# Latent attention: the values take the probabilities' low part last, two weight splits stand behind the heads, and the output projection begins within the last head

## The reference, cut to what matters

```python
def mla_attention(hn, w_dq, q_norm_g, w_uq, w_o, k_nope, k_rope, v, cos, sin):
    ...
        sc = (jnp.einsum('bqhd,bkhd->bhqk', qn, k_nope, preferred_element_type=jnp.float32)
              + jnp.einsum('bqhr,bkr->bhqk', qr, k_rope, preferred_element_type=jnp.float32)) * scale
        q_chunk = (start + jnp.arange(Q_BLOCK)) // CHUNK
        mask = key_chunk[None, :] <= q_chunk[:, None]
        sc = jnp.where(mask[None, None], sc, -jnp.inf)
        p = jax.nn.softmax(sc, axis=-1).astype(v.dtype)
        return jnp.einsum('bhqk,bkhd->bqhd', p, v)
    ...
    return o @ w_o
```

## Time and profile before

| | |
|---|---|
| median of 3 timed runs | 1744.71 us (1744.37 to 1747.96) |
| profiled execution, whole time | 1743.44 us |
| its span on the core | 1741.5 us |
| mean granted clock of TensorE | 0.997 |
| TensorE busy | 1711.8 us, 98% of the span |
| VectorE busy | 942.6 us, 54% |
| ScalarE busy | 608.1 us, 35% |

### The profile page before, as it was taken

The page is one execution under the profiler, slowest core; times in us unless marked ns, Lnnn a source line. Parts: engine busy times, 40 slices in busy tenths (PEclk is TensorE's granted clock), DMA queues, the critical chain, the costliest instruction groups (busy, mean ns, idle before and its releaser), DMA issues.

```text
span 1741.5 us, 21892 instructions
## 1 busy us (share of the span) xinstructions
PE 1711.8 (98%) x8088; PEld 1367.2 (79%) x8088; DVE 942.6 (54%) x1264; ACT 608.1 (35%) x894; POOL 185.2 (11%) x158
## 2 busy tenths in 40 slices
PE   9989999999999999999999999999999999999998
PEld 7768888888888866477888888888777788888886
DVE  5675546652665389857532343365873754234432
ACT  4553434431444232254321222243453432122221
POOL 0210211100111101110200011100000021001111
PEclk9999999999999999999999999999999999999999
DMA  6111223332223245311332323212211233322221
GB/s 231 62 53 56 85 82 97 96 121 88 93 87 107 84 136 158 100 63 59 121 97 97 93 92 97 94 60 86 72 37 34 74 109 98 97 86 96 97 83 48
DMA packets 48883, 157.84 MB, mean 91 GB/s; under 512 B 7088, under 2 KB 7728, under 8 KB 48816
## 3 DMA queue, kind: packets, MB, share of 16 engines
q1 hardware_dynamic: 48288, 155.45, 27.8%
q10 hardware_dynamic: 528, 1.46, 0.3%
HBM read 146.14 MB, written 2.10 MB: 85 GB/s over the span
## 4 chain that ended last, share of the span: by engine, by line
PE 90%; DVE 5%; ACT 2%; issue 1%; SPq 1%; DMA 0%; POOL 0%; DVEq 0%; ACTq 0%; POOLq 0%
PE bank L1133 26%; PE bank L1134 26%; PE bank L1135 26%; PE bank L1284 1%; PE bank L1669 1%; PE bank L1290 1%; PE bank L1285 1%; DVE cv L2281 1%; PE bank L1223 1%; DVE w_lo L1910 1%; SPq L484 1%; DVE swa_p L2013 1%; PE bank L1177 1%; PE bank L1839 1%; ACT w_hi L676 0%
## 5 line engine op out<-in xcount | busy, mean ns | idle before, releaser
L1910 DVE TENSOR_TENSOR w_lo<-w_raw,w_hi 128x1024 fp32r<-128x1024 f32 x269 | 347.3, 1292 | 313.0 <-ACT w_hi L676 190.1
L1133 PE MATMUL bank<-a_hi,w_hi 128*128 128x512 f32 x1156 | 460.6, 398 | 0.1
L1134 PE MATMUL bank<-a_lo,w_hi 128*128 128x512 f32 x1156 | 456.5, 395 | 0.0
L1135 PE MATMUL bank<-a_hi,w_lo 128*128 128x512 f32 x1156 | 454.3, 393 | 0.0
L1134 PE MATMUL bank<-g_lo,w_hi 128*128 128x512 f32 x688 | 272.0, 395 | 0.0
L1133 PE MATMUL bank<-g_hi,w_hi 128*128 128x512 f32 x688 | 270.8, 394 | 0.0
L1135 PE MATMUL bank<-g_hi,w_lo 128*128 128x512 f32 x688 | 269.0, 391 | 0.0
L1133 PEld LDWEIGHTS bank<-a_hi,w_hi 128*128 128x128 f32 x1156 | 218.1, 189 | 55.9 <-issue 6.0
L1135 PEld LDWEIGHTS bank<-a_hi,w_lo 128*128 128x128 f32 x1156 | 218.1, 189 | 48.5
L1134 PEld LDWEIGHTS bank<-a_lo,w_hi 128*128 128x128 f32 x1156 | 218.5, 189 | 46.4 <-issue 1.0
L676 ACT ACTIVATE w_hi<-w_raw 128x1024 fp32r<-128x1024 f32 x153 | 159.8, 1050 | 163.8 <-PE bank L1135 150.7
(11 more groups left out here) (290 smaller groups left out, 1807.6 us busy)
## 6 DMA issues: line engine op xcount, KB each, us to landing
w_raw<-in_stream SPq DMA_DIRECT2D x269, 512.0 KB, 3.5
shifted<-u_pad SPq DMA_DIRECT2D x120, 66.0 KB, 2.0
h<-in_xT SPq DMA_DIRECT2D x8, 256.0 KB, 5.5
out<-h SPq DMA_DIRECT2D x8, 256.0 KB, 2.1
cst_b<-in_consts SPq DMA_DIRECT2D x1, 896.0 KB, 9.7
cst_b<-in_consts ACTq DMA_DIRECT2D x1, 896.0 KB, 6.3
shifted<-u_pad ACTq DMA_DIRECT2D x8, 66.0 KB, 2.4
tap_cols<-in_vectors SPq DMA_DIRECT2D x16, 29.2 KB, 1.8
```

Source lines behind the costliest of these rows:

```text
L1133: pe.matmul(out, w0, x0, start=start, stop=False, skip_group_check=loose)
L1134: pe.matmul(out, w0, x1, start=False, stop=False, skip_group_check=loose)
L1135: return pe.matmul(out, w1, x0, start=False, stop=stop, skip_group_check=loose)
L1910: dve.tensor_tensor(w_lo[slot][:, :], w_raw[slot][:, :], f(w_hi[slot][:, :]), ALU.subtract)\
```

## The change

Three things are done. In `mla_values` the matmuls that read only `pt_hi` come first and wait for ScalarE's `pt_hi` parts (`mla_ea`); the four that read `pt_lo` come last and wait for VectorE's (`mla_ev`). The splits of the "wo" units 2 and 3 leave heads 1 and 2 and stand behind head 7. And tile 0 of the output projection is begun within head 7: slices 0 to 3 ahead of the transposes, slices 4 to 6 between these and the values; behind the values come slices 0 to 6 of tile 1, slice 7 of tile 0 and slice 7 of tile 1, then tiles 2 to 7 one after another.

```diff
@@ ScalarE
-                if i in (1, 2):
-                    w_hi_of(UNIT0["wo"] + i + 1, (UNIT0["wo"] + i + 1) % RING)
...
-            after("wo", "post1", 1, 1)
+            w_hi_of(UNIT0["wo"] + 2, (UNIT0["wo"] + 2) % RING)
+            after("wo", "post1", 1)
@@ TensorE
             def mla_values(i):
                 pe.wait_ge(x_ready, SPLIT0["mla"] + i)
+                w = slice(i * P, (i + 1) * P)
+                for kt in (0, 1, 3, 2):
+
+                    pe.wait_ge(mla_ea, 3 * i + mla_cols[kt][0] - 4)
+                    c = mla_cols[kt][2]
+                    pe.matmul(bank[4][:, kt * P:], T(v_hi, kt, MLA_H * V_DIM)[:, w], pt_hi[:, c:c + SEQ - kt * P],
+                              start=(kt == 0), stop=False, skip_group_check=True)
+                    pe.matmul(bank[4][:, kt * P:], v_lo(kt)[:, w], pt_hi[:, c:c + SEQ - kt * P],
+                              start=False, stop=False, skip_group_check=True)
                 for kt in (0, 1, 3, 2):
 
                     pe.wait_ge(mla_ev, 3 * i + mla_cols[kt][0] - 4)
                     c = mla_cols[kt][2]
-                    w = slice(i * P, (i + 1) * P)
-                    last = three(bank[4][:, kt * P:], T(v_hi, kt, MLA_H * V_DIM)[:, w], v_lo(kt)[:, w],
-                                 pt_hi[:, c:c + SEQ - kt * P], pt_lo[:, c:c + SEQ - kt * P], kt == 0, kt == 2, True)
+                    last = pe.matmul(bank[4][:, kt * P:], T(v_hi, kt, MLA_H * V_DIM)[:, w],
+                                     pt_lo[:, c:c + SEQ - kt * P], start=False, stop=(kt == 2), skip_group_check=True)
                 last.then_inc(mla_pv, 1)
+
+            def wo_part(j, k0, k1):
+
+                n = UNIT0["wo"] + j
+                if k0 == 0:
+                    unit_ready(n)
+                    pe.wait_ge(mla_exp, NB * (MLA_H - 1) + j + 1)
+                for k in range(k0, k1):
+                    k_ready("mla", k)
+                    last = three(bank[j][:, :], T(w_hi[n % RING], k, P), T(w_lo[n % RING], k, P),
+                                 T(mo_hi, k), T(mo_lo, k), k == 0, k == KD - 1)
+                if k1 == KD:
+                    last.then_inc(unit_used, 1)
...
+                else:
+                    wo_part(0, 0, 4)
                 mla_transpose(i)
                 if i + 1 < MLA_H:
                     mla_scores(i + 1, 3)
+                else:
+                    wo_part(0, 4, KD - 1)
                 mla_values(i)
-            tiles("wo", 8, mo_hi, mo_lo, "mla")
+            wo_part(1, 0, KD - 1)
+            wo_part(0, KD - 1, KD)
+            wo_part(1, KD - 1, KD)
+            for j in range(2, KD):
+                n = UNIT0["wo"] + j
+                unit_ready(n)
+                if j < 4:
+                    pe.wait_ge(mla_exp, NB * (MLA_H - 1) + j + 1)
+                else:
+                    bank_free("wo", j)
+                tile_of_eight(n, n % RING, bank[j % 4][:, :], mo_hi, mo_lo)
@@ VectorE
-                if i in (1, 2):
-                    lo_ahead(UNIT0["uv"] + i)
                 x_lo(SPLIT0["mla"] + i, mo_lo, mo_hi, i, bank[4][:, :])
+            lo_ahead(UNIT0["wo"] - 1)
             for k in range(KD):
                 n = UNIT0["wo"] + k
-                if k:
-                    lo_ahead(n)
+                lo_ahead(n)
                 unit_done(n)
```

## The result

The changed kernel takes 1728.69 us (median of 4 runs, 1727.27 to 1730.44); the kernel before took 1744.54 us (median of 4, 1742.32 to 1747.96). The ratio is 0.9908, 95% interval 0.9889 to 0.9927: 15.9 us faster, where 9.1 were forecast, and outside the range given. With more runs of both on one chip the ratio became 0.9955, 0.9940 to 0.9970, which is 7.8 us (5.2 to 10.4; experiment 5). So two things are to be explained: what the change gave, and where the other half of the first difference came from.

A forecast was written before the change was run, and what follows sets the result against it. TensorE carries 90% of the span, so only its stops and low clock can be won. 1.74 + 0.74 + 2.92 + 3.67 = 9.07 us off 1744.71 gives 1735.6 us, range 1732.8 to 1739.2.

The forecast's parts named there:

- Base: Whole kernel before: the median of three timed runs, 1744.71 us, is the time from which the gain is subtracted.
- Part 1: Values in the heads: taking pt_lo last wins 0.74 us in head 0 and 1.74 us over six periods.
- Rival A: Heads: VectorE's round sets the beat, periods stay at 7.25 us, 1.74 less gain, 1737.4 us; chance 12%.
- Part 2: Heads 1 and 2: moving two weight splits behind head 7 wins 2.92 us in the first three periods.
- The cover behind the heads: Behind head 7: the w_lo splits end 3.1 and 7.4 us before TensorE wants them, so moving them costs 0.
- T: End of head 7's values; the two w_lo were forecast to end at T + 3.1 and T + 4.3.
- Rival E: Behind the heads: the weights come late and the kernel gets slower; 1747.5 us with 15 us of delay; chance 3%.
- Part 3: Last head: output projection matmuls fill TensorE's waits and keep its clock up, winning 3.67 us; lower end 2.2.
- Rival B: Last head: the clock still falls for as long as before, 1.5 us less gain, 1737.1 us; chance 8%.
- Sum: Whole change: 1.74 + 0.74 + 2.92 + 3.67 = 9.07 us gained.
- C: Heads: transposes wait for the normalised rows instead, so only the tail is won, 1741.0 us; chance 6%.
- D: Heads: the change does not do what it says, for instance 32 added waits eat it; near 1744 us; chance 5%.

The follow-up runs named there:

- experiment 5: The changed kernel, unedited, run again with more timed runs: 1729.0 us against 1738.17 for the kernel before on the same chip, ratio 0.9955.
- experiment 1: The kernel before, unedited, profiled a second time: 1737.4 us (12 runs), ratio 0.9994 to the same program run beside it.
- experiment 6: The changed kernel with the values' old order, waiting for pt_lo at their head: 1732.08 us, ratio 0.9971.
- experiment 4: The kernel before with only the output projection begun inside head 7; values and splits as before: 1738.82 us, ratio 0.9991.
- experiment 7: The changed kernel with the two weight splits left in heads 1 and 2: 1733.48 us, ratio 0.9981.
- experiment 3: The kernel before with only the two weight splits moved behind head 7; TensorE as before: 1736.12 us, ratio 0.9984.
- 10: The kernel before with TensorE's loops of upA and upB written out: 1737.93 us (12 runs), ratio 0.9999.
- 2: The kernel before with only the values' new order, pt_lo last: 1735.29 us (11 runs), ratio 0.9984.

## Why the prediction was wrong

**Base (wrong, and this alone took it out of its range).** The prediction said: "The median of the three timed runs, 1744.71, lies 1.27 above it; I take the median as base." This took three runs and a profile that agree within 0.3% for the kernel's time. They were draws of one side: all four first runs of before lie at 1742.32 or more, where experiment 1 has its upper group, and all four of the changed kernel below 1731. The prediction's scatter of 1.5 us came from those runs, too. Over more runs the kernel before has medians of 1740.66, 1738.17 and 1737.19 us on three chips (34, 27 and 21 runs); from these the same 9.07 us lead to 1731.6, 1729.1 and 1728.1, where 1728.69 was measured. The step that failed is thus the base, taken too high by 4 to 7.5 us; the mechanism of the three parts is borne out below. The first profile held the sign: a pace of 233 ns from 250 to 607 us, and one of 229 ns elsewhere in the same trace.

**Part 1 (right).** Forecast 0.74 + 1.74. Head 0 gained 0.73; against experiment 6 the whole part is worth 2.95, because the period fell to 6.88 and not 6.96: the 12 values matmuls take 1.91 us (1301.59 to 1303.50), not 1.98. The prediction mis-sized the stop here: it took 1.98 for work, but the first matmul behind a stop is followed 0.31 us later, not 0.23. The second matmul of the values, before in head 5 and changed in head 6:

```profile
1304.96 0.39 PE L1134 MATMUL bank<-pt_lo,v_hi 128*128 128x512 f32 x1
...
1301.82 0.40 PE L1869 MATMUL bank<-pt_hi,a_hi 128*128 128x512 f32 x1
```

So a stop of 0.29 us in a head cost 0.37. The 0.10 us for the hand-over, for which the prediction has no row, was 0.11 (VectorE at 1260.10, values at 1260.21). Rival A is out, if narrowly. In the changed kernel VectorE's third maximum of head 7 still waits for TensorE, by 0.17 us, where it was 0.52 for head 6:

```profile
1299.26 0.56 DVE L2556 TENSOR_REDUCE small<-bank 128x1 f32<-128x384 f32 x1 [0.17 <-PE bank L1842]
```

The 4 added waits per head cost nothing that shows: in experiment 4, where head 7 has the old order with 4 waits and no stop ahead, its 12 matmuls take 1.91 us as well:

```profile
1322.89 0.40 PE L1133 MATMUL bank<-pt_hi,v_hi 128*128 128x512 f32 x1
...
1324.80 0.39 PE L1133 MATMUL bank<-mo_hi,w_hi 128*128 128x512 f32 x1
```

**Part 2 (right).** Forecast 2.92, measured 2.87 in the heads by itself, and 3.42 with the values' new order (experiment 7). The cover behind the heads is real: T + 3.05 in experiment 3 and T + 4.1 for both in the changed kernel, as worked out, and without the 27 matmuls of part 3 ahead of tile 2 the stop of 1.7 us is there. Rival E is out.

**Part 3 (right in size against the first profile).** Forecast 3.67, measured 3.86 (tail 52.53 to 48.67). But 1.6 of it is the low clock, which the kernel before has only in some executions: in 3 of the 5 profiles whose last head stands bare (before, experiments 3 and 10; not 1 and 2), and in none of the 8 with the projection inside it. Rival B is out: with matmuls round the ten transposes the clock stayed at 1.00. The rule of the Trainium skill on transposes (TensorE: Matmul & The Clock Gate, Part 4: PE-mode transpose) would let the dip survive there, and no run shows that. The steady worth of part 3 is 2.2 to 2.3 us.

**Sum.** Forecast 9.07, measured in the stretch 9.62 against the profile it was worked out from, and 8.05 against an execution without the low clock. The timed runs on one chip (ratio 7.8 us, 5.2 to 10.4; medians 9.2 us apart) fit both and do not decide between them. Rivals C and D are out.

**How the parts share it.** Alone, from a common base without the low clock, parts 1 and 3 give 2.75 and 2.2; part 2 gives 1.1, read between two profiles that both had the low clock. Together they give 8.05, 2 us more than the sum of 6.1. Part 3 takes away the stop that part 2 makes (1.7 us), and part 2 lets part 1 work in the first three heads, too.

## What to carry to other kernels

Work moved off a chain needs cover where it lands: moving the splits paid in full only together with the change that put 27 matmuls ahead of their first use. When a difference is small, match the two traces instruction by instruction and see whether the lead starts where the change is; here 4.5 us of it stood ahead of anything that was edited. And three times that agree are no distribution: a kernel can have two.

## What the runs showed of the hardware that was not expected

TensorE has two paces for the same stream of 128x512 fp32r matmuls at a granted clock of 1.00: starts 225, 230 and 231 ns apart, or all 233 ns. The slow pace began within a matmul of a tile boundary between 250 and 371 us (matmul 1375 to 1377 four times, 1807, 1857, 1905) and each time lasted to matmul 2906, where TensorE runs its first one-column sums behind the first block without standing still. It was absent in the other profiles, and never seen after that point in any of them. It costs up to 6.9 us of 1740. Times of 1741.5 us or more, where the upper group begins, came in 17 of 34, 1 of 27 and 3 of 21 runs of the kernel before on three chips. What starts it was not found: not the change, not a low clock, and not only the entry of a loop. Whether a stop would end it sooner is open, too.

The low clock in the last head does not follow from the stops alone. Experiment 1 has the same stops as the first profile, 5.25 us from the values of head 6 to those of head 7 in both, and kept a clock of 1.00.
